# Constant products in TensorE's waits, modulation blocks at heads 1, 3 and 5, and a split of the mixed features in four parts

## What is computed

```python
h = rms_norm(x, norm1_g[l])
proj = h @ w_in[l]
y_att = forgetting_attention(q, k, v, log_f)
y_conv = silu(layer_norm(causal_dwconv(a * sigmoid(gate)), g, b))
y_rnn = rglru(xr) * gelu(gate_in)
x = x + concatenate([y_att, y_conv, y_rnn]) @ w_out[l]
x = x + peer(rms_norm(x, norm2_g[l]), peer_wq[l], peer_k1[l], peer_k2[l], peer_u[l], peer_v[l])
```

## Time and profile before

| what | value |
|---|---|
| three timed runs | 3343.12, 3353.94, 3363.20 us; median 3353.94 |
| the profiled execution, its own time | 3341.9 us |
| span of the profiled execution | 3340.1 us |
| PE busy | 3202.3 us, 25032 products |
| DVE busy | 2208.7 us |
| ACT busy | 1394.3 us |
| POOL busy | 297.8 us |
| mean granted TensorE clock | 0.972 |
| moved by DMA | 478.55 MB, mean 143 GB/s |

### The profile page before, as it was taken

The page is one execution under the profiler, slowest core; times in us unless marked ns, Lnnn a source line. Parts: engine busy times, 40 slices in busy tenths (PEclk is TensorE's granted clock), DMA queues, the critical chain, the costliest instruction groups (busy, mean ns, idle before and its releaser), DMA issues. The chain is left out here.

```text
span 3340.1 us, 66418 instructions
## 1 busy us (share of the span) xinstructions
PE 3202.3 (96%) x25032; PEld 2793.0 (84%) x25032; DVE 2208.7 (66%) x4555; ACT 1394.3 (42%) x2184; POOL 297.8 (9%) x208
## 2 busy tenths in 40 slices
PE   7899999999999989999999999899999999999998
PEld 6699988989888869998998988776678877875998
DVE  6668886858985757797776897566532234667444
ACT  4444444353444444534344344444532223435443
POOL 1247000000000225600000000000000000000000
PEclk9899999999999989999999999899989999899999
DMA  7645445464446753545445445320022222221453
GB/s 267 238 138 169 158 155 175 149 189 151 151 161 202 258 197 127 195 146 173 162 160 183 147 151 173 123 89 32 3 71 98 95 95 88 97 91 36 137 182 118
DMA packets 131691, 478.55 MB, mean 143 GB/s; under 512 B 14512, under 2 KB 16560, under 8 KB 130992
## 3 DMA queue, kind: packets, MB, share of 16 engines
q1 hardware_dynamic: 115696, 416.72, 37.1%
q0 software_dynamic: 15808, 59.25, 5.2%
HBM read 474.87 MB, written 1.05 MB: 142 GB/s over the span
## 5 line engine op out<-in xcount | busy, mean ns | idle before, releaser
L1475 DVE TENSOR_TENSOR Wl<-ring,Wh 128x1024 fp32r<-128x1024 f32 x700 | 856.5, 1224 | 843.9 <-ACT Wh L1035 842.6
L490 PE MATMUL bank<-HR,Wh 128*128 128x256 f32 (+1 forms) x8192 | 1284.5, 310 | 40.9 <-DVE HR L2046 18.9
L490 PEld LDWEIGHTS bank<-HR,Wh 128*128 128x128 f32 x8192 | 1127.8, 193 | 127.5 <-issue 55.8
L1035 ACT CAST Wh<-ring 128x1024 fp32r<-128x1024 f32 x788 | 824.6, 1046 | 751.1 <-PE bank L490 743.2
L490 PE MATMUL bank<-HR,Wl 128*128 128x256 f32 (+1 forms) x4096 | 658.1, 303 | 0.0
L490 PEld LDWEIGHTS bank<-HR,Wl 128*128 128x128 f32 x4096 | 576.6, 193 | 29.5
L490 PE MATMUL bank<-Wh,HR 128*128 128x512 f32 x2304 | 578.7, 394 | 2.7 <-DVE HR L1800 2.7
L490 PEld LDWEIGHTS bank<-Wh,HR 128*128 128x128 f32 x2304 | 426.8, 188 | 94.7 <-issue 5.5
L490 PE MATMUL bank<-arena 128*128 128x32 bf16 (+4 forms) x7144 | 413.1, 204 | 32.1 <-issue 11.3
L490 PEld LDWEIGHTS bank<-arena 128*128 128x128 bf16 (+3 forms) x7144 | 301.0, 108 | 131.8 <-issue 57.1
L1235 ACT ACTIVATE arena<-bank 128x256 f32 (+1 forms) x256 | 98.6, 385 | 504.9 <-PE bank L490 504.8
(11 more groups left out here) (232 smaller groups left out, 1786.3 us busy)
## 6 DMA issues: line engine op xcount, KB each, us to landing
ring<-weights SPq DMA_DIRECT2D x788, 512.0 KB, 3.3
HA<-mods POOLq DMA_DIRECT2D x96, 512.0 KB, 6.6
arena<-bias POOLq DMA_DIRECT2D x16, 256.0 KB, 2.9
arena<-keys POOLq DMA_DIRECT2D x2, 1024.0 KB, 6.1
arena<-mla POOLq DMA_DIRECT2D x1, 1536.0 KB, 6.5
K<-constants SPq DMA_DIRECT2D x1, 1402.0 KB, 6.1
X<-x SPq DMA_DIRECT2D x1, 1024.0 KB, 8.6
X<-context POOLq DMA_DIRECT2D x1, 1024.0 KB, 7.6
```

What stands on the lines that cost most here:

```text
L490: return nc.tensor.matmul(out, lhsT, rhs, start=first, stop=last)
L1035: nc.scalar.copy(Wh[:, i % SPL], ring[:, i % RAW]).then_inc(S("hi_done"), 1)
L1475: v.tensor_tensor(Wl[:, i % SPL], ring[:, i % RAW], Wh[:, i % SPL], ALU.subtract).then_inc(S("lo_done"), 1)
```

## The change

It has three parts.

1. `keep_clock(n, b)` issues n products of a constant (the ones, read as bf16, 128 columns of weights and 512 moving columns) into PSUM bank b, whose content nobody needs at that place. It is called at 29 places of the executed program, 212 products in all: 4 and 5 in heads 0 and 1, 10 behind modulation block 10, 4 and 3 around the sums of n2 (each in both layers); 26 ahead of the spread of fin; 3 and 8 around the spread of a0; 6, 3 and 8 at a1; 4, 3 and 8 at f0 and at f1; 7 and 4 + 6 at the start of the attentions; 17 ahead of the second products of either layer, and 16 and 9 between their halves.
2. `MOD_HEADS` becomes `{1: 7, 3: 8, 5: 9}`.
3. The mix is split in four parts, (6, 7), (0, 1, 2), (3) and (4, 5), each as soon as it is there: ACT makes the high parts at pass 6, at pass 8, behind the root and behind the SiLU, DVE the low parts in the same order. The first output tile takes its chunks in that order and waits for each part apart; its entry waits only for the root, and the `mod_add` of blocks 7 to 9 moves behind the last low part.

```diff
-MOD_HEADS = {1: 7, 4: 8, 7: 9}
+MOD_HEADS = {1: 7, 3: 8, 5: 9}
...
+        MIX_PARTS = ((6, 7), (0, 1, 2), (3,), (4, 5))
+        OUT_ORDER = [c for p in MIX_PARTS for c in p]
...
+            onesb = k("ones").bitcast(BF16)
+            onesw = onesb.unsqueeze(1).broadcast_to([P, 2, 2 * P])
+
+            def keep_clock(n, b):
+
+                for _ in range(n):
+                    mm(b[:, :], onesb[:, 0:P], onesw, True, True)
...
+                    if h < 2:
+                        keep_clock(4 + h, bank[3])
...
                 mod_turn(l, 9)
                 mod_block(l, 10)
-
-                pe.wait_ge(S("y_ev"), 4 * (l + 1))
-                pe.wait_ge(S("ln_out"), 2 * (l + 1))
-                pe.wait_ge(S("rnn_out"), l + 1)
-                pe.wait_ge(S("h_out"), SPLITS[f"m{l}"][1])
+                keep_clock(10, bank[7])
+
+                pe.wait_ge(S("ln_root"), l + 1)
                 for m_ in range(N_OUT):
+                    if m_ == 3:
+                        pe.wait_ge(S("mod_out"), 3 * l + 2)
                     if m_ >= 4:
                         pe.wait_ge(S("op_ev"), N_OUT * l + m_ - 3)
-                    feature_tile(t0 + N_IN + m_, bank[m_ % 4][:, 0:T], *Hx)
+                    feature_tile(t0 + N_IN + m_, bank[m_ % 4][:, 0:T], *Hx, order=OUT_ORDER,
+                                 ready=None if m_ else lambda c: SPLITS[f"m{l}"][0] + 1 + [c in p for p in MIX_PARTS].index(True))
                     if m_ >= 2:
                         norm_sums(f"n2.{l}", m_ - 2, 1)
 
+                keep_clock(4, bank[4])
                 norm_sums(f"n2.{l}", C - 2, 2)
+                keep_clock(3, bank[4])
                 norm_spread(f"n2.{l}")
...
             norm_sums("fin", 0, C)
+            keep_clock(26, bank[5])
             norm_spread("fin")
...
+                        if n == 1:
+                            keep_clock(7, bank[7])
                         if 1 <= n <= 32:
                             transpose_unit(n - 1, 2 if (n - 1) % 4 < 2 else 4)
...
+                keep_clock(17, bank[4])
                 pe.wait_ge(S("hid"), KF * (l + 1))
                 for half in range(2):
+                    if half:
+                        keep_clock(16 if l == 0 else 9, bank[0])
...
+                def mix_high(p):
+
+                    cs = MIX_PARTS[p]
+                    nc.scalar.copy(Hh[:, cs[0]:cs[-1] + 1, XS], mixT[:, cs[0]:cs[-1] + 1, :]).then_inc(S("h_hi"), 1)
...
+                    if h == 7:
+                        mix_low(0)
+                mix_low(1)
+                mix_low(2)
                 dve.wait_ge(S("ln_root"), l + 1)
...
-                split_low(f"m{l}", [(Hl[:, c:c + 4, XS], mixT[:, c:c + 4, :], Hh[:, c:c + 4, XS]) for c in (0, 4)])
+                mix_low(3)
+                mod_add(l, *MODS[1])
```

More of the change, by code:

```diff
@@ L422, in build @@
         _n = 0
-        for name_, pieces in (("n1.0", 4), ("m0", 2), ("n2.0", 4), ("n1.1", 4), ("m1", 2), ("n2.1", 4),
+        for name_, pieces in (("n1.0", 4), ("m0", 4), ("n2.0", 4), ("n1.1", 4), ("m1", 4), ("n2.1", 4),
                               ("c0", 8), ("a0", 8), ("m2", 5), ("f0", 16), ("a1", 16), ("m3", 4), ("f1", 8)):
@@ L518, in norm_spread, with feature_tile @@
                 m.then_inc(S("norm_bc"), 1)
-            def feature_tile(i, out, mh, ml, it=0, ready=None):
+            def feature_tile(i, out, mh, ml, it=0, ready=None, order=range(C)):
                 w = high(i, it)
-                for c in range(C):
+                for n, c in enumerate(order):
                     if ready:
                         pe.wait_ge(S("h_out"), ready(c))
-                    mm(out, w[:, c, :], mh[:, c, :], c == 0, False)
+                    mm(out, w[:, c, :], mh[:, c, :], n == 0, False)
                     mm(out, w[:, c, :], ml[:, c, :], False, False)
@@ L847, in _ @@
                 else:
+                    keep_clock(6, bank[4])
                     norm_sums("a1", 4, 4)
+                keep_clock(3, bank[4])
                 norm_spread(f"a{l}")
+                keep_clock(8, bank[0])
                 if l == 0:
@@ L971, in _ @@
                                        lambda i, h=h: vN[:, i, h * HD:(h + 1) * HD])
+                        if n == 33:
+                            keep_clock(6, bank[1])
                         if 33 <= n <= 64:
@@ L1155, in _ @@
                             nc.scalar.copy(mixT[:, g // 2, :], bank[(g // 2) % 2][:, 0:T]).then_inc(S("y_ev"), 1)
+                    if h == 6:
+                        act.wait_ge(S("rnn_out"), l + 1)
+                        mix_high(0)
                     if h == HEADS:
@@ L1162, in _ @@
                     .then_inc(S("ln_root"), 1)
+                act.wait_ge(S("y_ev"), 4 * (l + 1))
+                mix_high(2)
                 act.wait_ge(S("ln_z"), l + 1)
@@ L1166, in _ @@
                         .then_inc(S("ln_out"), 1)
-                act.wait_ge(S("rnn_out"), l + 1)
-                act.wait_ge(S("y_ev"), 4 * (l + 1))
                 act.wait_ge(S("ln_out"), 2 * (l + 1))
-                split_high(f"m{l}", [(Hh[:, c:c + 4, XS], mixT[:, c:c + 4, :]) for c in (0, 4)])
+                mix_high(3)
                 mod_evac(l, 10)
@@ L1636, in _, with mix_low @@
                 dve.wait_ge(S("bc_ev"), 5 * (l + 1))
+                def mix_low(p):
+                    cs = MIX_PARTS[p]
+                    dve.wait_ge(S("h_hi"), SPLITS[f"m{l}"][0] + p + 1)
+                    v.tensor_tensor(Hl[:, cs[0]:cs[-1] + 1, XS], mixT[:, cs[0]:cs[-1] + 1, :], Hh[:, cs[0]:cs[-1] + 1, XS],
+                                    ALU.subtract).then_inc(S("h_out"), 1)
                 for h in range(HEADS + 1):
```

4 lines of the change are left out of this document (3 added, 1 removed).

## The result

| what | before | after |
|---|---|---|
| timed runs, same chip | 3351.28 us median (3343.12 to 3363.2, 4 runs) | 3315.43 us median (3313.19 to 3318.1, 4 runs) |
| ratio | | 0.9893, interval 0.9867 to 0.9919 |
| the profiled execution, its own time | 3341.9 us | 3318.1 us |
| its span | 3340.1 us | 3316.3 us |
| mean granted TensorE clock | 0.972 | 0.987 |

The change takes 1.1% off the time: 3315 us against 3310 predicted. The two profiled executions lie only 23.8 us apart, though, and the medians 36. So the 38.3 us that the prediction worked out for the profiled execution came out as 23.8, and part of why the forecast still fits is scatter.

The account below looks back on a forecast made before the run. PE, busy 96%, was taken to bound the kernel, with 184.3 us at low clock. Rearrangement 14 plus clock terms 24.3 made 38.3 off 3341.9, so 3303.6; half of the 12 us median offset on top gave 3310, range 3290 to 3332.

Parts of the forecast that it names:

- the rearrangement: End of the mixer's heads: block 9 at head 5 and the split mix start the output projection earlier; 7 per layer, 14 us.
- The term of the second products: Feed-forward: groups of 17, 16, 17 and 9 products let the tiles behind them run at full clock; 8.9 us.
- norm 2: Second norm of the mixer, both layers: 4 and 3 products shorten block 11; 1.25 us per layer, 2.5 in all.
- f1: Norm f1: first tile fed by DVE, so sums, spread and products behind the tile come back; estimated 1.5 us.
- the neighbourhood attention: 10 products in two waits ahead of its loop speed up ten scores and the transposes; 2.2 us.
- The slower rival: Constant products don't count for the clock and cost 0.43 us each; net 27 us slower, 3369 or 3375; chance 0.04.
- the rival of the long fills: Only long fills work, short ones don't hold the clock; 21.5 us gained, 3320.4 or 3326; chance 0.18.
- The rival of the transfers: Blocks 8 and 9 wait for weights and the heads stretch by what the end gains; 3317.6 or 3324; chance 0.09.
- The nine products per layer in heads 0 and 1: Mixer heads: the 4 and 5 constant products there gain nothing, since DVE sets the pace; 0 us.
- The waits for transfers: Heads: blocks 8 and 9 each wait about 0.6 us for weights, scores come up to 0.8 late; 0.8 taken off.
- Join: Join of the two blocks: 26 products overrun by 1.4, sums, spreads and first tile speed up; net 3.9 us (1 to 5).
- Norms a1 and f0: Norms with DVE-fed first tiles: sums, spread and products behind the tile come back; estimated 3.5 and 1.3 us.

Follow-up runs that it names:

- e1: The changed kernel with no constant product at all, only the rearrangement left; 3343.12 us, ratio 0.9982 to before.
- e3: The changed kernel with only the groups of 9 and more products, those of 3 to 8 gone; 3331.91 us, ratio 0.9951 to before.
- e0: The changed kernel itself run again, unchanged, as the control on another chip; 3318.48 us, ratio 0.9899 to before.
- e2: The kernel before with the 212 products at the places of the change and nothing else; 3330.36 us, ratio 0.9948 to before.
- e9: The changed kernel plus 256-column products inside modulation blocks 7 to 9 only, 21 per layer; 3315.24 us, ratio 0.9893 to before.
- e6: The changed kernel without the nine products in heads 0 and 1; 3324.83 us, ratio 0.9911 to before.
- e5: The changed kernel with modulation blocks 7, 8, 9 at heads 1, 4 and 7 again; 3319.89 us, ratio 0.992 to before.
- e7b: The kernel e7 run again on another chip; 3312.82 us, ratio 0.9888 to before.
- e7: The changed kernel with more fills: inside blocks 7 to 9, in sums of c0 and fin, latent attention, n1, join; 3315.33 us, ratio 0.9891 to before.
- e8: The kernel e7 with the modulation blocks back at heads 1, 4 and 7; 3321.78 us, ratio 0.9913 to before.
- e4: The changed kernel with products of zeros in place of ones, same shapes and counts; 3320.61 us, ratio 0.992 to before.

## Why the prediction was right, and where it was wrong

**What held.** The kernel was bound by PE, and the clock was the larger part (0.5% for the products alone, 0.2% for the rearrangement). The products count for the clock, run 0.22 us apart and cover the waits. The term of the second products came out at 8.9 of 8.9 us, norm 2 at 2.6 of 2.5, f1 at 1.7 of 1.5, the neighbourhood attention at 2.9 of 2.2. These terms are no accident of one execution. In all ten profiles with all the groups at these places f1 took 20.0 us and the neighbourhood attention 95.0, against 21.6 to 21.7 and 97.7 to 98.1 in before, e1 and e3; the first two stages of the second products took 16.6 and 15.7 us in the ten and in e3, against 18.8 and 18.6, and 19.3 and 17.2, in before and e1. The slower rival fell with the first row of 17 products in 3.84 us, the rival of the long fills with e3. The rival of the transfers did not come true in after; where it seems to in e0 (second layer 57.5 us, before 56.0), the time lies under 27.3 us of low clock, not in the waits themselves (0.58 and 0.69 us at block 7). The Trainium skill ("TensorE: Matmul & The Clock Gate", "Why this matters for your kernels") makes the loss of the clock a matter of long idle gaps. The traces don't agree: no wait longer than 0.77 us stands close ahead of the low stretches of 10 and 31 us in the heads of after and e2.

**The reason that failed: "The nine products per layer in heads 0 and 1 are worth nothing: DVE sets the pace."** The pace of DVE was read in a window at full clock. At the 1.2 GHz level PE needs 4.02 us for a head's scores and transposes and is the slower one; e2 shows DVE waiting 5.32 us for it. The heads are therefore not outside the clock's reach. A low stretch in them does not pay in full either: 27.3 us of it made the second layer's heads 8.9 us longer (e0 against e9, 57.5 and 48.6), a third of its length, where PE work that doubles its time would make it half. Whether the nine products themselves are worth something is not settled by e6.

**The rearrangement, 10.5 of 14.** Layer 0 gave 6.3 us, near the 7, but by e5 more through the split of the mix than through the move of block 9. The second layer gave 4.2, and in the control's profile nothing (57.5 against 56.0 before). The waits for transfers were forecast at 0.6 us for blocks 8 and 9 and came out at 0.58 and 0.85 in the first layer and at 0 and 1.10 in the second. Block 7, for which none was forecast, waits 0.93 and 1.35. Their direct price was near, and what a low clock in the heads costs was left out; that the waits cause it stays a guess.

**Join, 1.2 of 3.9.** The timeline of PE in after:

```profile
2141.76 7.85 PE L492 MATMUL bank<-K 128*128 128x512 bf16 x26
2149.45 0.61 PE L492 MATMUL bank<-K,col 128*128 128x128 f32 x4
...
2151.08 5.42 PE L492 MATMUL bank<-K,arena 128*128 128x2 f32 x32 [0.90 <-ACT arena L1047]
```

The 26 products took 7.85 us, against 7.5 in the working. But the clock fell again at 2152.8, in the middle of 32 tiny products, and the sums of a0 took 5.42 us instead of the 3.7 that the term had counted. The fill raised the clock and didn't hold it across the 2-column products behind it. In e7b four more products stand directly ahead of these sums, and the same row is short (in e7 and e8 too, 3.73 us). The single products among the sums of fin ahead of them did not hold the clock: those sums ran at half (1.71 us for eight at 2141.92, where the first eight of c0 took 1.03).

```profile
2151.93 1.03 PE L492 MATMUL bank<-K 128*128 128x512 bf16 x4
...
2153.12 3.73 PE L492 MATMUL bank<-K,arena 128*128 128x2 f32 x32
```

The stage took 52.2 us there and in e7, but 53.3 in e8, whose program is the same here.

**Norms a1 and f0, 1.4 and 0 of 3.5 and 1.3.** The first tile at f0 before and after, PE's timelines (pairs from its middle):

```profile
2473.90 1.22 PE L490 MATMUL bank<-HR,Wh 128*128 128x512 f32 x2 [0.36 <-DVE HR L1882]
2475.48 1.22 PE L490 MATMUL bank<-HR,Wh 128*128 128x512 f32 x2 [0.35 <-DVE HR L1882]
```
```profile
2463.62 0.73 PE L492 MATMUL bank<-HR,Wh 128*128 128x512 f32 x2 [0.79 <-DVE HR L1931]
2465.19 0.73 PE L492 MATMUL bank<-HR,Wh 128*128 128x512 f32 x2 [0.84 <-DVE HR L1931]
```

The pairs start 1.58 us apart at either clock: DVE's low parts pace them, and a faster PE only waits longer. The prediction said so, but counted the spread and the products behind the tile as won. In after the spread is at half clock again (2457.59, 1.92 us), and so is the end of the tile. In no profile did f0 come out below the 34.9 us of before. At a1 the execution decides as well: it took 25.3 to 25.4 us in six of the ten profiles with all the groups, 27.0 in e7 and e8, and 23.3 in e2 and e4, which is the forecast's 3.5 us below before.

**The median against the profile.** I put 6 us on the sum for executions unluckier than the profiled one. The medians are 36 us apart, near the 38.3 worked out, and the profiles 23.8. The difference is where the two profiled executions lie: before's is 9.4 us below its median, after's 2.7 above. So the sum for the profiled execution missed by 14.5 us, and that 3310 lies within 5 us of the measured median is in part luck. The five us of the attentions are chance, by e0 and e5. That the rest of the gap is chance too is likely but not shown: no profile belongs to the median execution.

## What to carry to other kernels

When an engine that "doesn't bind" has two speeds, work out its pace at the lower one before calling a stage covered. Waits of about a microsecond were worth filling here where slow work stood behind them (groups of 3 to 8 gave 0.3 to 0.5%), and a constant's product into a free bank delayed nothing where it ended before the release. Judge such a change over several executions: stages whose program is unchanged moved by up to 6.6 us from one profile to the next, by where the clock fell.

## What the runs showed of the hardware

- **A low clock can last where PE is fully busy.** In e0 it held for 23.9 us with PE busy for all of them, in e2 for 30.7 us with PE busy for 30.1, over scores of 64 rows and blocks of 32 columns of the array; in e1 it rose after 20.5 us over the same kind of work. What ends such a stretch stays open.
- **Products of zeros hold the clock too**, with no difference from ones that the runs can tell.
- **The scatter of this kernel's executions.** Kernels with none of the products or only the long groups spread over 16 to 22.5 us (before, e1 and e3, 4 to 22 executions each), most of those with all of them over 5 to 12 us in four to six executions. Two fall out of that: e2 with 15.4 us and e5 with 24.5, of which one execution at 3337.53 makes up more than half. e6, without the nine products in the heads, spreads over 20.
- **Waits alone don't tell where the clock falls.** Transfer waits of 0.65 and 0.70 us stand directly ahead of a low stretch of 10.2 us in the second layer of after, and waits of 0.23 and 0.70 us at the same place of its first layer have full clock behind them.
